# Up projection of the middle groups by seven block products, with activation sums streamed from DRAM

## What is computed

```python
def squared_relu_mlp(h, w_up, w_down):
    return jnp.square(jax.nn.relu(h @ w_up)) @ w_down
...
        ff = squared_relu_mlp(rmsnorm(h, norm_mlp_pre[l]), w_mlp_up[l], w_mlp_down[l])
        h = h + rmsnorm(ff, norm_mlp_post[l])
```

## Time and profile before

| | us |
|---|---|
| median of 3 runs | 2319.8 (2318.87 to 2319.85) |
| the profiled execution | 2321.57 |
| its span, first to last instruction | 2319.7 |
| PE busy | 2280.9 (98%) |
| DVE busy | 1402.4 (60%) |
| ACT busy | 622.8 (27%) |
| POOL busy | 654.7 (28%) |
| moved by DMA | 144.98 MB, mean 62 GB/s |
| granted TensorE clock, mean | 0.997 |

### The profile page before, as it was taken

One profiled execution on the slowest core, in us unless ns is written; L12 is line 12 of the kernel. 1 busy time (PEld: TensorE's weight loads), 2 busy tenths in 40 slices (PEclk: granted clock), 3 DMA queues, 4 the chain that ended last, 5 costly groups with the idle time before them and its releaser, 6 DMA issues.

```text
span 2319.7 us, 33213 instructions
## 1 busy us (share of the span) xinstructions
PE 2280.9 (98%) x13712; PEld 2072.8 (89%) x13712; DVE 1402.4 (60%) x1438; ACT 622.8 (27%) x756; POOL 654.7 (28%) x387
## 2 busy tenths in 40 slices
PE   8999999999999999999999999999999999999997
PEld 7999989999999999999989999877788888888887
DVE  6788544633745745746587886355437456646768
ACT  4564433420111111110254653232301111111112
POOL 3333215023213213222414332151232232233240
PEclk9999999999999999999999999999999999999999
DMA  3011002322111111111241111033211121111113
GB/s 135 33 59 37 28 28 92 99 70 69 41 54 63 45 54 63 45 54 46 83 139 46 51 37 37 19 100 87 77 65 55 43 72 63 36 63 64 44 57 144
DMA packets 57323, 144.98 MB, mean 62 GB/s; under 512 B 5136, under 2 KB 24848, under 8 KB 57232
## 3 DMA queue, kind: packets, MB, share of 16 engines
q1 hardware_dynamic: 32816, 109.06, 14.2%
q10 hardware_dynamic: 24416, 34.60, 4.7%
...
## 4 chain that ended last, share of the span: by engine, by line
PE 87%; DVE 7%; ACT 3%; issue 2%; DMA 0%; DVEq 0%; POOL 0%; SPq 0%; ACTq 0%; POOLq 0%
PE banks L678 54%; PE banks L903 17%; PE banks L809 5%; PE banks L730 2%; PE banks L733 1%; PE banks L718 1%; PE banks L717 1%; PE banks L1002 1%; PE banks L1009 1%; DVE hid L2007 1%; PE banks L958 1%; PE banks L979 1%; PE banks L1080 1%; PE banks L1017 1%; ACT sum_hi L1459 1%
## 5 line engine op out<-in xcount | busy, mean ns | idle before, releaser
L678 PE MATMUL banks<-X,w_hl 128*128 128x348 f32 (+2 forms) x6624 | 1192.2, 340 | 2.4 <-ACT ki L1387 1.8
L678 PEld LDWEIGHTS banks<-X,w_hl 128*128 128x128 f32 x6624 | 1096.8, 188 | 80.6 <-issue 7.6
L530 POOL TENSOR_SCALAR w_hl<-w_raw 128x1024 fp32r<-128x1024 f32 x70 | 90.1, 1288 | 803.8 <-issue 549.0
L903 PE MATMUL banks<-sum_hi,w_hl 128*128 128x260 f32 (+1 forms) x1152 | 247.0, 319 | 0.0
L1450 ACT ACTIVATE hid<-hid 128x1044 f32<-128x1044 f32 (+1 forms) x48 | 51.4, 1070 | 704.1 <-DVE hid L1995 704.1
L532 POOL TENSOR_TENSOR w_hl<-w_raw,w_hl 128x1024 fp32r<-128x1024 f32 x70 | 202.6, 2894 | 5.8
L903 PE MATMUL banks<-sum_hi,w_third 128*128 128x260 f32 (+1 forms) x864 | 192.4, 323 | 6.5 <-DVE Y L2024 6.5
L903 PEld LDWEIGHTS banks<-sum_hi,w_hl 128*128 128x128 f32 x1152 | 178.0, 188 | 17.0
L1995 DVE SCALAR_TENSOR_TENSOR hid<-banks,rs 128x1044 f32<-128x1044 f32 (+1 forms) x48 | 59.3, 1235 | 207.9 <-PE banks L678 207.9
L903 PEld LDWEIGHTS banks<-sum_hi,w_third 128*128 128x128 f32 x864 | 135.7, 188 | 21.5 <-DVE Y L2024 7.7
L2024 DVE TENSOR_TENSOR Y<-banks,Y 128x520 f32<-128x520 f32 (+1 forms) x144 | 122.0, 867 | 52.2 <-PE banks L903 51.5
...
## 6 DMA issues: line engine op xcount, KB each, us to landing
w_raw<-w_units SPq DMA_DIRECT2D x160, 512.0 KB, 3.5
r<-w_units SPq DMA_DIRECT2D x36, 512.0 KB, 4.7
...
h_old<-h_out ACTq DMA_DIRECT2D x8, 512.0 KB, 4.4
h_mid<-Y ACTq DMA_DIRECT2D x8, 512.0 KB, 5.3
```

The source lines that it names most:

```text
L530: nc.gpsimd.tensor_scalar(slot[:, 0], w_raw[:, s], 1.0, 1.0, ALU.mult, ALU.mult).then_inc(w_rounded, 1)
L678: ins = nc.tensor.matmul(out[:, b, 0:t.width(b)], wp, xp[:, t.used(b)], start=first and n == 0, stop=last and n == 2)
L903: ins = nc.tensor.matmul(out[:, m + b, :], wp, xp[:, k, cols], start=k == 0 and i == 0, stop=k == 1 and i == 2)
```

## The change

In the middle groups of both layers the up projection too is done by seven block products. The weights' quarters (512 rows by 256 columns) are combined into sums like the down weights; the activation's sums T1 to T4 are made once per layer. For this, group 0 gets `scale_x`, `x_sums`, `round_t`, `x_low` and `store_lows` on ACT and DVE, and 16 stores to `t_mem` (DRAM), after four stores that save B12 (the second token half of X's first four tiles) to `b12_mem`. In each middle group SP loads the halves of T1..T4 back into three places; places 0 and 1 lie over B12, which is loaded again at the end of the last middle group. Each load of a half is two DMAs, high and low part.

The products run on PE in the order UP_1, UP_5, UP_6, UP_3, UP_7, UP_2, UP_4 and accumulate in two chains of PSUM banks: chain 0 takes 1, 6, 7 and 4, chain 1 takes 5 and 3, then 2. After some of them ACT copies the chain's state to `hid` (`copied`), and DVE finishes the quarters with three `up_sum`s; the chain goes on accumulating. `up_done` counts the products, `t_half_used` the first halves of 5, 6, 7 and 4. All fourteen weight operands of a group are rounded by POOL (1 instruction) and their low parts made by DVE (`weights_low`); the first of the next group (UP_A11) is prepared at the end of the group, for group 1 behind `y_spread`. The down products come in another order (X_B22, X_T3, X_B11, ...). SP, POOL and DVE now run five groups in the loop and the last one written out. The diff, cut to its core (indents shortened): constants, then SP, POOL, PE, ACT, DVE.

```diff
+(UP_A11, UP_S1, UP_S2, UP_S4, UP_S3, UP_A12, UP_A22,
+ DN_S4, DN_S3, DN_A11, DN_S1, DN_S2, DN_A12, DN_A22) = range(OPERANDS)
+W_SLOT = (0, 1, 2, 0, 1, 2, 0, 1, 2, 0, 1, 2, 0, 1)
+W_RAW = (0, 2, 0, 2, 1, 3, 2, 2, 0, 2, 1, 3, 0, 2)
...
+    def when_split(operand):
+        sp.wait_ge(wpart_ready, OPERANDS * n + operand + 1)
+    sp.wait_ge(t_half_used, 4 * n + 1)
+    t_load(l, 0, T2, 1)
+    when_split(UP_S2)
+    sp.wait_ge(wsum_made, WEIGHT_SUMS * n + SUM_UP_S4 + 1)
+    raw_load(l, g, 0, 1, Q_A21)
+    when_split(UP_S4)
+    raw_load(l, g, 2, 0, Q_A22)
+    sp.wait_ge(up_done, products + UP_5 + 1)
+    t_load(l, 1, T3, 0)
+    sp.wait_ge(t_half_used, 4 * n + 2)
+    t_load(l, 2, T3, 1)
+    when_split(UP_S3)
+    raw_load(l, g, 1, 1, Q_A22)
+    sp.wait_ge(up_done, products + UP_6 + 1)
+    t_load(l, 0, T4, 0)
+    when_split(UP_A12)
+    raw_load(l, g, 3, 1, Q_A11)
+    when_split(UP_A22)
+    raw_load(l, g, 2, 1, Q_A12)
+    sp.wait_ge(t_half_used, 4 * n + 3)
+    t_load(l, 1, T4, 1)
+    if not last:
+        sp.wait_ge(up_done, products + UP_7 + 1)
+        t_load(l, 2, T2, 0)
+    when_split(DN_S4)
+    raw_load(l, g, 2, 1, Q_A11)
+    when_split(DN_S3)
+    raw_load(l, g, 0, 1, Q_A12)
+    for place, used in ((0, (t_half_used, 4 * n + 4)), (1, (up_done, products + PRODUCTS))):
+        sp.wait_ge(*used)
+        if not last:
+            t_load(l, place, T1, place)
+            continue
+        for s in range(2):
+            sp.dma_start(t_slot(l, place, s).bitcast(f32), b12_part(l, place, s)).then_inc(b12_loaded, 16)
+    when_split(DN_A11)
+    raw_load(l, g, 2, 1, Q_A22)
+    if not last:
+        when_split(DN_S1)
+        raw_load(l, g + 1, 1, 0, Q_A21)
+        when_split(DN_S2)
+        raw_load(l, g + 1, 3, 0, Q_A12)
+        when_split(DN_A12)
...
+    sp.wait_ge(mm_done, FIRST + done(l, j_up(0, GT - 1)))
+    sp.wait_ge(t_stored, 16 * 20 * (l + 1))
+    for place in range(2):
+        t_load(l, place, T1, place)
+    sp.wait_ge(mm_done, FIRST + done(l, j_down(0, 7)))
+    raw_load(l, 1, 2, 0, Q_A22)
+    t_load(l, 2, T2, 0)
+    raw_load(l, 1, 3, 0, Q_A12)
...
-    rounded(l, g, W_S3, products(3))
-    rounded(l, g, W_A22, products(4))
-    up(4, products(5))
-    up(5, products(6))
...
+    rounded(l, g, UP_S4, ups(1))
+    rounded(l, g, UP_S3, ups(2))
+    rounded(l, g, UP_A12, ups(3))
+    rounded(l, g, UP_A22, ups(4))
+    rounded(l, g, DN_S4, ups(5))
+    rounded(l, g, DN_S3, ups(6))
+    rounded(l, g, DN_A11, ups(7))
+    rounded(l, g, DN_S1, products(1))
+    rounded(l, g, DN_S2, products(2))
+    rounded(l, g, DN_A12, products(3))
+    rounded(l, g, DN_A22, products(4))
+    if last:
+        split_pair(l, units_before_last() // 2, products(6), group_done(l, g))
+    else:
+        rounded(l, g + 1, UP_A11, products(6))
+def group_done(l, g):
+    return lambda: pool.wait_ge(mm_done, FIRST + done(l, j_down(g, 7)))
...
+        if idx == UP_1:
+            pe.wait_ge(ps_free[m], FIRST + l * SET_JOBS[m] + J_MLP // 2 + 6 * g)
+        elif m == 0 and idx == UP_5:
+            pe.wait_ge(part_added, added)
+        elif m == 0 and idx == UP_2:
+            pe.wait_ge(up_summed, 3 * n + 1)
+        elif m == 0:
+            pe.wait_ge(up_copied, 4 * n + {UP_6: 1, UP_3: 2, UP_7: 3, UP_4: 4}[idx])
+    def halves_of_t(idx):
...
+    if before is not None:
+        pe.wait_ge(part_added, added + t.place(before))
+    elif t.chain_of(t.pairs[job]) == 0:
+        pe.wait_ge(relu_made, 4 * n + 4)
+    elif t.chain_of(t.pairs[job]) == 1:
+        pe.wait_ge(up_summed, 3 * n + 3)
...
+    act.wait_ge(mm_done, FIRST + done(l, J_O + 7))
+    scale_x(0)
+    hidden(0, 0, l * COUNTED_TILES)
+    hidden(0, 1, l * COUNTED_TILES)
+    round_t(0)
+    hidden(0, 2, l * COUNTED_TILES)
+    store_lows(0)
+    hidden(0, 3, l * COUNTED_TILES)
+    act.wait_ge(t_stored, 16 * (20 * l + 12))
+    scale_x(1)
+    round_t(1)
+    store_lows(1)
...
+    when_summed(g, SUM_UP_S1)
+    weights_sum(g, SUM_UP_S3, 1, 0, 1, ALU.subtract)
+    when_summed(g, SUM_UP_S3)
+    weights_sum(g, SUM_UP_S2, 0, 2, 0, ALU.subtract)
+    weights_low(g, UP_S1)
+    when_loaded(g, 3, 1)
+    when_summed(g, SUM_UP_S2)
+    dve.wait_ge(wpart_ready, operands_before(l, g) + UP_S1 + 1)
+    weights_sum(g, SUM_UP_S4, 2, 3, 0, ALU.subtract)
+    weights_low(g, UP_S2)
+    weights_low(g, UP_S4)
+    weights_low(g, UP_S3)
+    when_loaded(g, 0, 2)
+    when_loaded(g, 1, 2)
+    weights_sum(g, SUM_DN_S1, 1, 0, 1, ALU.add)
+    weights_low(g, UP_A12)
+    dve.wait_ge(up_done, PRODUCTS * n + UP_3 + 1)
+    dve.wait_ge(up_copied, 4 * n + 3)
+    up_sum(0, (0, 1), None)
+    relu(0, (0, 1))
+    when_loaded(g, 3, 2)
+    when_summed(g, SUM_DN_S1)
+    weights_sum(g, SUM_DN_S3, 0, 3, 0, ALU.subtract)
+    when_summed(g, SUM_DN_S3)
+    weights_sum(g, SUM_DN_S2, 3, 1, 3, ALU.subtract)
+    weights_low(g, UP_A22)
+    dve.wait_ge(up_copied, 4 * n + 4)
+    up_sum(1, (1, 1), (1, 0))
+    when_loaded(g, 2, 3)
+    when_summed(g, SUM_DN_S2)
+    weights_sum(g, SUM_DN_S4, 2, 2, 3, ALU.subtract)
+    relu(1, (1, 1))
+    weights_low(g, DN_S4)
+    dve.wait_ge(act_sq, l * F_TILES + g * GT + 2)
+    hidden_difference(t3[:, :, 0:t.width], b22, b12)
+    dve.wait_ge(up_done, PRODUCTS * n + UP_2 + 1)
+    up_sum(2, (0, 0), None)
+    low(X_B22, b22)
+    relu(2, (0, 0))
+    weights_low(g, DN_S3)
+    low(X_T3, t3[:, :, 0:t.width])
+    dve.wait_ge(up_done, PRODUCTS * n + UP_4 + 1)
+    V.scalar_tensor_tensor(out=by_up_blocks(l, b21), in0=up_banks(l, 0), scalar=0.0, in1=by_up_blocks(l, half_rs(l, 0)),
+                           op0=ALU.max, op1=ALU.mult).then_inc(relu_made, 1)
+    add_half(0)
+    dve.wait_ge(act_sq, l * F_TILES + g * GT + 3)
+    dve.wait_ge(xsum_made, 4 * n + SUM_T3 + 1)
+    hidden_difference(b12, b12, b11)
+    weights_low(g, DN_A11)
...
+    add_half(1)
+    low(X_B11, b11)
+    add_half(2)
+    weights_low(g, DN_S1)
+    dve.wait_ge(xsum_made, 4 * n + SUM_T1 + 1)
+    hidden_difference(b22, b22, b12)
+    add_half(3)
+    low(X_T1, b12)
+    add_half(4)
+    weights_low(g, DN_S2)
+    add_half(5)
+    low(X_T2, b22)
+    add_half(6)
+    weights_low(g, DN_A12)
+    add_half(7)
+    low(X_B21, b21)
+    add_half(8)
+    dve.wait_ge(xsum_made, 4 * n + SUM_T2 + 1)
+    dve.wait_ge(xpart_lo, PRODUCTS * n + X_B21 + 1)
+    hidden_difference(b21, b21, b22)
+    weights_low(g, DN_A22)
+    add_half(9)
+    low(X_T4, b21)
+    add_half(10)
+    if not last:
+        first_up_sum(g + 1)
+    add_half(11)
+    if not last:
+        weights_low(g + 1, UP_A11)
+    add_half(12)
+    add_half(13)
 def sum_parts(i):
...
+    dve.wait_ge(t_summed, before + 1)
+    from_x(made[T2], second, made[T1], ALU.subtract)
+    dve.wait_ge(t_summed, before + 3)
+    from_x(made[T4], first, made[T2], ALU.subtract)
+def x_low(half, part):
...
+    dve.wait_ge(t_stored, 16 * 20 * (l + 1))
...
-    with dve.Fori(1, GROUPS - 1) as g:
-        middle_group(g)
+    weights_low(1, UP_A11)
+    first_up_sum(1)
+    with dve.Fori(1, MIDDLE) as g:
+        middle_group(g, False)
+    middle_group(MIDDLE, True)
```

493 lines of the change are left out of this document (296 added, 197 removed).

## The result

The changed kernel takes 2392.0 us against 2319.8: 1.032 times the time before, 95% interval 1.030 to 1.033, 72 us slower. The forecast was 2409 us, with 2335 to 2450 around it. The profiled execution has a span of 2390.1 us, 70.4 us over the span before.

The account below looks back on a forecast made before the run. Before, TensorE (98% busy) bounds; afterwards queued loads and a DVE chain delay each group's down products. Layer 0 groups 24, layer 1 groups 16, starts 23, group 0 2, clock 24: 89 us slower, 2409 us, range 2335 to 2450.

Parts of the forecast that it names:

- Raw 1: Load of down quarter A22 in the up half, queued behind other loads: lands at 24.0 us, in layer 1 23.2.
- the chain from there to the first down product: Up half, from A22's landing: DVE work, reloads and POOL roundings without slack, 23.0 us; first down product at 47.0 or 46.2.
- Rival (a): Whole kernel: PE's saving counts and the order holds; groups gain 51 us, less 25 at the starts, 2294 us; chance 0.08.
- Layer 1's groups: Six middle groups of layer 1: 46.2 + 39.0 + 0.8 = 86.0 us each, +2.6 a group, 16 us for six.
- Layer 0's groups: Six middle groups of layer 0: 47.0 + 42.0 + 2.8 = 91.8 us each, +4.0 a group, 24 us for six.
- The starts: Before each layer's middle groups: PE stands 11.3 us for UP_A11's low part, queued on DVE; 23 us for both layers.
- Group 0: First group of each layer: x_sums(1) delays a down_sum past when PE wants its banks, 1 us a layer, 2 us.
- The clock: Half clock after idle PE, 1.7 us lost once per place, twelve middle groups and two starts: 14 x 1.7 = 24 us.
- What would show it: Signs in the new profile: PE idle before first down product, DVE's 9 us load wait, 11 us idle at starts.
- (b): Middle groups: POOL and DVE meet less than counted and the clock holds; chain 20 us, total 2340 us; chance 0.15.
- (c): Load queue slower, nearer 230 GB/s: A22 lands 7 us later, 84 us more, up to 2490 us; chance 0.12.
- (d): Matmul count: not seven eighths, PE's count would show it; time near 2319.8 us; chance 0.01.

Follow-up runs that it names:

- The bytes experiment: Changed kernel, same order, but each load of an activation sum in the middle groups moves only 8 of its 520 or 512 columns: 2333.6 us.
- the best order: Raw 2 issued ahead of T3's second half, first down_sum inside x_sums(1), against a kernel already reordering loads, DVE, starts and port (2304.1 us): 2271.1 us.
- the first experiment: Against the changed kernel, SyncE issues T4's second half ahead of the wait for UP_A22's split and the load of raw 2: 2395.9 us.
- the last experiment: Against the 2271.1 us kernel, the roundings of DN_S4 and DN_S3 are made by POOL again instead of ACT: 2292.7 us.

## Why the prediction was right
**The sign and the mechanism.** Raw 1 was forecast 24.0 us into a group of layer 0 and landed at 23.8; the chain from there to the first down product was forecast to end at 47.0 and ended at 46.5, the product started at 47.7. That the chain's length fits, 22.7 us for 23.0, is in part luck: the forecast had POOL's rounding of DN_S3 ahead of the difference T3, 2.2 us, and it came ahead of low DN_S4, so that the difference took 1.2 us and low DN_S4 with its wait 3.0 where 2.3 were forecast; and sum DN_S1 took 1.6 us beside a rounding where an undisturbed one takes 1.2. The bytes experiment confirms the cause: without the backlog raw 1 is 4.4 us earlier and 58 us of the 72 are gone. Raw 1's landing alone does not decide it: landing at 17.9, with raw 3 late behind it, it left the time at 2386. Rival (a)'s price for the groups, 51 us gained, is met by the best order in sum, 496.0 and 480.7 us, 50.5 less than before, but not in its parts: layer 0 gains 30.7 us where (a) had 19, layer 1 19.8 where it had 32. The best order also has more changed than (a) assumed, so this agreement is luck. It mends most of the starts and of group 0 as well, so it ends at 2271 and not at 2294.

**Layer 1's groups.** 2.6 us a group and 1.7 for the clock, 25.8 us for six; measured 21.6, 4.2 less.

**Layer 0's groups: this term was mis-sized.** 4.0 us a group and 1.7 for the clock, 34.2 us for six; measured 16.9, so 17.3 too much. The mean of the six groups is 90.6 us, where the prediction with its clock had 93.5. The up half, its half clock included, takes 47.6 (forecast 47.0), the down half 43.0 (forecast 42.0 + 2.8), and nothing comes on top for the clock. The step that failed is "the down products 336 in 42.03 us", taken as pure matmul time at 125.1 ns: the earlier trace rows has TensorE busy for 40.93 of them, so 1.1 us was a wait already, as the prediction itself had noted. The best order does 336 matmuls of 260 columns in 40.16 us, 119.5 ns each. The wait for relu 3 was also smaller, 1.3 to 2.3 us in place of 2.8; in two of the six groups half clock stands behind it, and these down halves take 44.2 and 44.5 us. By the rule of the Trainium skill that the prediction cited ("TensorE: Matmul & The Clock Gate", section "Wait — 56ns, not 53.3ns?") a matmul would take 110.8 ns; the trace lies between that and the prediction's 125.1, and the trace decides.

The 17.3 us are as much as the whole distance between the forecast of 89 us and the 72 measured, but only because the other misses cancel: layer 1's groups and the clock at the two starts were forecast 7 us too high together, and group 0 7 us too low.

**The starts.** 22.6 us forecast and 3.4 for the clock, 23.3 measured in the gaps: TensorE waits for DVE's w_hl, 11.5 us, in both layers. But the time to be had back there is smaller, 5 to 7 us a layer, since raw 2's load is next late. A wait's length is the cost of what made it only until the next late thing; whoever repairs it needs the second number.

**Group 0.** 2 us forecast, 9.1 measured. x_sums(1) starts 1.6 us later than reckoned, for the rescaling on ACT, and takes 6.1 us instead of 5.2, because its 520-wide operations take about 0.75 us and one of them 1.5. TensorE's gap is 3.5 us in layer 0 and 2.1 in layer 1, and in layer 0 half clock stands behind it. The 1.7 us for the clock here was not in my count of fourteen places.

**The clock.** 24 us forecast, taken once per place with the work behind it. The stretches show a mean granted clock of 0.96 and 0.97 over the groups, and 0.54 in the 5.09 us behind the T4 gap: 2.2 us lost there. What that costs in the end can't be read off. VectorE's chain ends 46.5 us into this group and TensorE is there at 47.7, so about 1.2 of the 2.2 us show and the rest is covered by the chain; and the first experiment moves the gap in front of the down products and leaves the time within 4 us of what it was. Where nothing covers it, as in the two down halves of the last experiment, it costs 1.4 us a place, near the 1.7 that I took. No run priced the clock alone in the kernel after; its share of the groups' 38 us stays open.

**Which wait.** "What would show it" named PE's idle time before the first down product, released by sum_lo, and said that this wait covers the late T4 half. It is the reverse: the T4 half stands in the queue behind raw 2, which is issued only after raw 3 has been used, and lands at 42.6 us, not at about 41, so PE meets this wait first, and sum_lo is ready 1 us before PE is. I had taken T4's half for a load of its own; it hangs on the same chain. The other signs held: VectorE's wait for w_raw 9.7 us (9 forecast), raw 1's load 8.2 us to landing, the wait for hid, 1.3 to 2.3 us in layer 0, DVE busy 67.6 us in the group shown, against 66.

**The other rivals.** (b), a cheaper meeting of POOL and DVE, is out: the chain took 22.7 us against 23.0 forecast and 20 in (b). Two POOL roundings taken off it are worth 20.8 us on the long chain and 21.6 on the short one, 1.7 to 1.8 us a group. (c), a slower queue, is out: the plateau stands at about 400 GB/s against 398 in the earlier trace rows. The 358 GB/s that the Trainium skill gives ("DMA: Bandwidth & Descriptors", Specifications) would by the prediction's estimate have put raw 1 at 25.3 us; it came at 23.8, and the measurement decides. (d) is out: 13856 matmuls are those of seven products in both layers, 13712 + 6 x 48 - 6 x 24.
